# Five upward projections of a two-layer hybrid network as seven quarter products per pair of weight blocks

## What is computed

```python
D_MODEL, SEQ, D_FF = 1024, 512, 4096
def hybrid_layer(x, ...):
    ...
    x = x + merged @ w_o
    h2 = rmsnorm(x, norm_mlp)
    return x + jnp.square(jax.nn.relu(h2 @ w_up)) @ w_down
```

## Time and profile before

| what | value |
|---|---|
| median of 3 runs | 2454.3 us (2454.13 to 2454.35) |
| span of the profiled execution | 2451.9 us |
| PE busy | 2440.2 us, 11368 matmuls |
| DVE / ACT / POOL busy | 1275.7 / 839.2 / 1369.9 us |
| HBM read | 244.17 MB |

### The profile page before, as it was taken

One profiled execution on the slowest core, in us unless ns is written; L12 is line 12 of the kernel. 1 busy time (PEld: TensorE's weight loads), 2 busy tenths in 40 slices (PEclk: granted clock), 3 DMA queues, 4 the chain that ended last, 5 costly groups with the idle time before them and its releaser, 6 DMA issues.

```text
span 2451.9 us, 33111 instructions
## 1 busy us (share of the span) xinstructions
PE 2440.2 (100%) x11368; PEld 1997.5 (81%) x11368; DVE 1275.7 (52%) x1813; ACT 839.2 (34%) x1099; POOL 1369.9 (56%) x1672
## 2 busy tenths in 40 slices
PE   9999999999999999999999999999999999999999
PEld 7888888888888888888888888888777777888887
DVE  7884412355655658844123535437876565733333
ACT  5332232231111223312322312114577775422222
POOL 6556655556766655566555666656432334555554
PEclk9999999999999999999999999999999999999999
DMA  5223332343344332233333433443211212332322
GB/s 192 83 69 98 99 94 94 94 150 127 118 146 146 94 95 86 68 96 94 95 102 95 146 119 125 149 154 95 76 50 42 61 40 70 95 103 87 103 93 93
DMA packets 64887, 247.46 MB, mean 101 GB/s; under 512 B 7200, under 2 KB 9888, under 8 KB 63520
## 3 DMA queue, kind: packets, MB, share of 16 engines
q1 hardware_dynamic: 62496, 218.13, 28.8%
q10 hardware_dynamic: 2304, 28.17, 2.9%
HBM read 244.17 MB, written 2.10 MB: 100 GB/s over the span
## 4 chain that ended last, share of the span: by engine, by line
PE 68%; POOL 16%; issue 12%; DVE 2%; ACT 1%; DVEq 0%; DMA 0%; POOLq 0%; SPq 0%; ACTq 0%
PE ps L586 63%; POOL w_lo L521 16%; PE ps L873 1%; PE ps L886 1%; PE ps L902 1%; PE ps L841 1%; ACT prob L1377 0%; PE ps L906 0%; PE ps L702 0%; DMA w_raw<-weights 0%; DVE sq_q L2036 0%; PE ps L856 0%; DVE A_hi_f L1632 0%; ACT prob L1383 0%; PE ps L778 0%
## 5 line engine op out<-in xcount | busy, mean ns | idle before, releaser
L521 POOL TENSOR_TENSOR w_lo<-w_raw,w_hi 128x256 fp32r<-128x256 f32 x1608 | 1324.4, 855 | 988.4 <-ACT w_hi L1122 855.3
L586 PE MATMUL ps<-H_hi,w_hi 128*128 128x512 f32 x1936 | 767.0, 396 | 0.3 <-DVE H_lo L1987 0.2
L586 PE MATMUL ps<-H_hi,w_lo 128*128 128x512 f32 x1936 | 754.0, 389 | 0.0
L586 PE MATMUL ps<-H_lo,w_hi 128*128 128x512 f32 x1936 | 753.8, 389 | 0.0
L1122 ACT ACTIVATE w_hi<-w_raw 128x1024 fp32r<-128x1024 f32 x399 | 420.3, 1056 | 894.4 <-PE ps L586 864.3
L586 PEld LDWEIGHTS ps<-H_hi,w_hi 128*128 128x128 f32 x1936 | 363.5, 188 | 81.9 <-issue 9.1
L586 PEld LDWEIGHTS ps<-H_lo,w_hi 128*128 128x128 f32 x1936 | 363.6, 188 | 77.2 <-issue 4.5
L586 PEld LDWEIGHTS ps<-H_hi,w_lo 128*128 128x128 f32 x1936 | 363.4, 188 | 76.7
L586 PE MATMUL ps<-A_lo,w_hi 128*128 128x512 f32 x552 | 214.8, 389 | 0.0
L586 PE MATMUL ps<-A_hi,w_hi 128*128 128x512 f32 x496 | 193.0, 389 | 0.0
L586 PE MATMUL ps<-A_hi,w_lo 128*128 128x512 f32 x496 | 193.0, 389 | 0.0
(11 more groups left out here) (291 smaller groups left out, 2929.1 us busy)
## 6 DMA issues: line engine op xcount, KB each, us to landing
w_raw<-weights SPq DMA_DIRECT2D x403, 512.0 KB, 3.6
mod_w<-mod_weights ACTq DMA_DIRECT2D x8, 3072.0 KB, 12.5
toeplitz<-biases SPq DMA_DIRECT2D x14, 128.0 KB, 2.1
out<-X SPq DMA_DIRECT2D x7, 256.0 KB, 2.0
X<-x SPq DMA_DIRECT2D x3, 512.0 KB, 7.8
decay_sb<-decay ACTq DMA_DIRECT2D x1, 1024.0 KB, 7.2
ctx_sb<-context ACTq DMA_DIRECT2D x1, 1024.0 KB, 15.6
X<-x SPq DMA_DIRECT2D x2, 256.0 KB, 4.3
```

The costliest lines, as they stand in the source:

```text
L521: last = nc.gpsimd.tensor_tensor(lo[:, c:c + LOW_COLS], w_raw[:, q, c:c + LOW_COLS], hi[:, c:c + LOW_COLS].bitcast(F32), ALU.subtract)
L586: mm = nc.tensor.matmul(dst, w[l], xs[r], start=start and a == 0, stop=stop and a == 2)
```

## The change

In the five groups (0,1), (0,2), (0,3), (1,1) and (1,2) the eight up jobs become four pairs. The two weight blocks of a pair are a matrix of 2x2 quarters (two output tiles by two halves of the contraction: `A11`, `A12` from the first block, `A21`, `A22` from the second), and `H` is one as well (two halves of the contraction by two halves of the tokens). The pair's product is made from seven quarter products in place of eight (Winograd's form of Strassen's method). A quarter product is 4 tiles times 3 matmuls of 128x256. It needs:

- four sums of weight quarters, `S1` to `S4`, 128x512 each, on DVE (`sum_of`); each of the seven pieces `A11 S3 S2 S4 A12 S1 A22` is rounded by ACT and its low part is made by POOL (five of them, `piece_lows`) or DVE (`S1`, `S3`, `sum_low`);
- four sums of quarters of `H`, `T1` to `T4`, made once for each layer during the up jobs of the group (L,0) (`t_step`): DVE does one 128x1024 difference, twelve 128x256 sums and four 128x1024 low parts, ACT eight 128x256 scalings and four 128x1024 roundings. They lie where `C` was, so that all groups but (1,3) now write to `A`;
- three copies out of PSUM or within it by ACT for each pair (`copy_first`, `keep_second`, `keep_third`, 128x256), and on DVE two 128x256 additions, two instructions that apply relu and `rstd`, and two low parts; the squares move from DVE to ACT (four 128x512 instructions for each pair).

The product of a pair lies in banks n mod 4, the next one, and bank 4 or 7 (`THIRD_BANK`). Since bank 7 is among the banks of the transposes, PE now waits for `mod_reduced` before the first quarter product of such a group. The pieces of the group's first pair are made during the down jobs of the group before (`first_pair`), in the ring slots that those jobs give free. The code and data of the other stages stay.

```diff
+FAST = ((0, 1), (0, 2), (0, 3), (1, 1), (1, 2))
+FAST_JOBS = {L * LAYER_JOBS + JOB_FF + g * FF_GROUP_JOBS + 2 * j: (L, g, j)
+             for L, g in FAST for j in range(DT // 2)}
...
+        def free_of(engine, piece, n):
+            j, i = FAST_JOBS[n][2], PAIR_OF[n]
+            if j == 0:
+                engine.wait_ge(jobs_done, n + place(piece, i) // 2 + 1)
+            elif piece == "S4":
+                engine.wait_ge(jobs_done, n + 2)
+            else:
+                engine.wait_ge(piece_used[piece], i)
...
+            def piece_lows(piece, n):
+                i = PAIR_OF[n]
+                s = place(piece, i)
+                whole = raw_of(piece, n) if piece[0] == "A" else set_lo_f[:, s, :]
+                if piece == "S2":
+                    pool.wait_ge(piece_summed["S4"], i + 1)
+                if piece == "A22":
+                    pool.wait_ge(w_hi_ready, n + 2)
+                else:
+                    pool.wait_ge(piece_high[piece], i + 1)
+                for c in range(0, V_WIDE, LOW_COLS):
+                    last = nc.gpsimd.tensor_tensor(set_lo[:, s, c:c + LOW_COLS], whole[:, c:c + LOW_COLS],
+                                                   set_hi[:, s, c:c + LOW_COLS].bitcast(F32), ALU.subtract)
...
+            def quarter(piece, n, dst, B, start=False):
+                i = PAIR_OF[n]
+                s = place(piece, i)
+                if piece == "A22":
+                    pe.wait_ge(w_lo_ready, n + 2)
+                else:
+                    pe.wait_ge(piece_low[piece], i + 1)
+                for k in range(HALF_K):
+                    cols = slice(k * P, (k + 1) * P)
+                    mm = product(dst, (set_hi[:, s, cols], set_lo[:, s, cols]), B(k), start and k == 0, k == HALF_K - 1, True)
...
+                if part == 1:
+                    pe.wait_ge(bank_free, n + 2)
+                    quarter("A11", n, c11, B11, start=True)
+                elif part == 7:
+                    quarter("S3", n, c21, T(T3), start=True)
+                elif part == 6:
+                    pe.wait_ge(first_copied, i + 1)
+                    quarter("S2", n, c12, T(T2))
+                elif part == 2:
+                    pe.wait_ge(first_copied, i + 1)
+                    quarter("A12", n, c11, B21)
+                elif part == 5:
+                    pe.wait_ge(second_kept, i + 1)
+                    quarter("S1", n, c12, T(T1))
+                elif part == 4:
+                    pe.wait_ge(third_kept, i + 1)
+                    quarter("A22", n, c21, T(T4))
+                else:
+                    pe.wait_ge(c22_added, i + 1)
+                    quarter("S4", n, c12, B22)
...
+                    if (L, g) in FAST:
+                        if g == 1:
+                            pe.wait_ge(t_ready, 4 * (L + 1))
+                        pe.wait_ge(mod_reduced, L * FF_GROUPS + g)
+                        pairs = [ng + 2 * j for j in range(DT // 2)]
+                        for j, m in enumerate(pairs):
+                            fast_pair(m, 1)
+                            fast_pair(m, 7)
+                            if j:
+                                fast_pair(m - 2, 4)
+                            fast_pair(m, 6)
+                            if j:
+                                fast_pair(m - 2, 3)
+                            fast_pair(m, 5 if j == DT // 2 - 1 else 2)
+                            fast_pair(m, 2 if j == DT // 2 - 1 else 5)
+                        fast_pair(pairs[-1], 4)
+                        fast_pair(pairs[-1], 3)
+                        down_part(ng + DT, 0, 6, hi, lo, ready)
+                        down_part(ng + DT + 1, 0, 6, hi, lo, ready)
+                        down_part(ng + DT, 6, DT, hi, lo, ready)
+                        down_part(ng + DT + 1, 6, DT, hi, lo, ready)
...
+                def t_diffs():
+                    V.tensor_tensor(T_lo_f[:, T1, :, :], X[:, 0:HALF_K, HALF_T:S], X[:, 0:HALF_K, 0:HALF_T],
+                                    ALU.subtract).then_inc(diff_ready, 1)
+                def t_sums(t):
+                    dve.wait_ge(diff_scaled, 2 * L + (1 if t == T3 else 2))
+                    fence()
+                    half = slice(0, HALF_T) if t == T4 else slice(HALF_T, S)
+                    for k in range(HALF_K):
+                        last = V.scalar_tensor_tensor(out=T_lo_f[:, t, k, :], in0=X[:, HALF_K + k, half],
+                                                      scalar=column(PAR_NORM2 + HALF_K + k, L),
+                                                      in1=T_lo_f[:, {T3: T3, T2: T1, T4: T2}[t], k, :],
+                                                      op0=ALU.mult, op1=ALU.subtract)
+                    last.then_inc(t_whole, 1)
+                def t_lows(t):
+                    dve.wait_ge(t_high, 4 * L + (2, 3, 1, 4)[t])
+                    V.tensor_tensor(T_lo[:, t, :, :], T_lo_f[:, t, :, :], T_hi[:, t, :, :].bitcast(F32),
+                                    ALU.subtract).then_inc(t_ready, 1)
+                def t_step(s):
+                    if s == 0:
+                        t_diffs()
+                    elif s == 1:
+                        t_sums(T3)
+                    elif s == 2:
+                        t_sums(T2)
+                        t_lows(T3)
+                    elif s == 3:
+                        t_sums(T4)
+                        t_lows(T1)
+                    elif s == 5:
+                        t_lows(T2)
+                    elif s == 6:
+                        t_lows(T4)
...
+                def sum_of(piece, n):
+                    i = PAIR_OF[n]
+                    s = place(piece, i)
+                    a11, a12 = (w_raw[:, n % RING, h * V_WIDE:(h + 1) * V_WIDE] for h in range(2))
+                    a21, a22 = (w_raw[:, (n + 1) % RING, h * V_WIDE:(h + 1) * V_WIDE] for h in range(2))
+                    if piece == "S3":
+                        for b in range(n, n + 2):
+                            dve.wait_ge(w_loaded[b % RING], (b // RING + 1) * 16)
+                    else:
+                        fence()
+                    free_of(dve, piece, n)
+                    a, b, op = {"S3": (a11, a21, ALU.subtract), "S2": (a22, set_lo_f[:, place("S3", i), :], ALU.subtract),
+                                "S4": (a12, set_lo_f[:, place("S2", i), :], ALU.subtract),
+                                "S1": (a21, a22, ALU.add)}[piece]
+                    V.tensor_tensor(set_lo_f[:, s, :], a, b, op).then_inc(piece_summed[piece], 1)
+                def sum_low(piece, n):
+                    i = PAIR_OF[n]
+                    s = place(piece, i)
...
+                def add_c22(n):
+                    i = PAIR_OF[n]
+                    dve.wait_ge(third_kept, i + 1)
+                    dve.wait_ge(piece_used["S1"], i + 1)
+                    V.tensor_tensor(second_out[:, HALF_T:S], ps[:, n % RING + 1, 0:HALF_T], kept[:, 1, :],
+                                    ALU.add).then_inc(c22_added, 1)
...
+                def second_of(n):
+                    i = PAIR_OF[n]
+                    dve.wait_ge(piece_used["A22"], i + 1)
+                    V.tensor_tensor(second_out[:, 0:HALF_T], ps[:, THIRD_BANK[i % 2], 0:HALF_T], kept[:, 0, :],
+                                    ALU.add).then_inc(c21_added, 1)
+                    fence()
+                    V.scalar_tensor_tensor(out=E[:, 1, :], in0=second_out[:, :], scalar=0.0, in1=rstd[:, :],
+                                           op0=ALU.max, op1=ALU.mult).then_inc(bank_free, 1)
...
+                def first_of(n):
+                    q = n % RING
+                    dve.wait_ge(jobs_done, n + 2 + RING)
+                    V.scalar_tensor_tensor(out=halves(E[:, 0, :]), in0=ps[:, q:q + 2, 0:HALF_T],
+                                           scalar=0.0, in1=halves(rstd[:, :]), op0=ALU.max,
+                                           op1=ALU.mult).then_inc(bank_free, 1)
...
+                def fast_low(n, t):
+                    m = 2 * FAST_JOBS[n][2] + t
+                    dve.wait_ge(e_squared, 2 * PAIR_OF[n] + 2 - t)
+                    V.tensor_tensor(A_lo[:, m, :], Alf[:, m, :], A_hi[:, m, :].bitcast(F32),
+                                    ALU.subtract).then_inc(tiles_ready, 1)
...
+                def fast_up(n0):
+                    for j in range(DT // 2):
+                        n = n0 + 2 * j
+                        more = j + 1 < DT // 2
+                        if j:
+                            add_c22(n - 2)
+                            sum_of("S1", n)
+                        if more:
+                            sum_of("S3", n + 2)
+                        if j:
+                            sum_low("S1", n)
+                            second_of(n - 2)
+                        if more:
+                            sum_of("S2", n + 2)
+                            sum_of("S4", n + 2)
+                            sum_low("S3", n + 2)
```

(22 more changed lines are left out.)

258 lines of the change are left out of this document (239 added, 19 removed).

## The result

The changed kernel takes 2495.0 us (median of 4 runs, 2493.8 to 2495.9) against 2454.3 of the kernel before: ratio 1.0167 [1.0152, 1.0181]. The prediction was 2488.0, in 2460 to 2510, slower with 0.86. The span of the profiled execution is 2491.7 us, 39.8 more than before.

What follows compares the result with a forecast made beforehand. The prediction took the kernel to be bound by TensorE's (PE's) stream. On the profiled 2451.9 us, -17.7 + 21.1 + 17.5 + 13 = +33.9 gave a 2485.8 us span, 2488.2 with the runs' extra 2.4; range 2460 to 2510.

Steps and rivals of the forecast that it cites:

- The gain: PE in the 20 pairs: 84 narrow matmuls in place of 48 wide ones save 0.88 us a pair, 17.7 us.
- The rival that ended faster: Quarter products: matmuls under 0.113 us apart would make the kernel faster, 2443.6 us at 0.1067; chance 0.07.
- The wait at the start: Start of the five groups: PE waits for `mod_reduced` behind DVE's added `S1` work, 4.3 or 4.1 us each, 21.1 us.
- DVE inside the up stage: Middle pairs: DVE needs 11.5 us against PE's 10.00 and falls behind; stalls of 3.5 us a group, 17.5 us.
- The prediction's own sign of being wrong: It is wrong if PE does not idle at group starts, or DVE has a free microsecond in the middle pairs.
- The `T` sums: (0,0) and (1,0): DVE's seventeen added instructions make PE stall in its first down job, 6.5 us a layer, 13 us.
- The clock: Rival: granted clock falls to 1.2 GHz for as long as each of five holes lasts, +10.5 us, 2499; chance 0.14.
- DVE keeps pace: Rival: two-input DVE instructions take 0.69 us throughout, only the start waits stay whole, 2464.5 us; chance 0.22.

Runs made afterwards that it cites:

- e11_load_in_gap: Changed kernel with PE's start wait one pair later, `T` low parts and `T4` in down stages, steps reordered, `mod_w` load after the last up block's work: 2443.5 us.
- b2_hole_long: Kernel before, with PE waiting for the reductions at five group starts and DVE's first reduction done three times over: 2485.0 us.
- e4_half_pool: Changed kernel with POOL making only half of the low part of its five pieces, PE using that half twice: 2485.3 us.
- e8_load_last: Changed kernel with PE's start wait one pair later, `T` low parts in down stages, two order swaps, `mod_w` load at the last pair: 2463.7 us.
- b1_hole_short: Kernel before, with PE waiting for DVE's reductions at the start of the same five groups, products as they were: 2466.1 us.
- e1_wait_later: Changed kernel with PE's wait for the reductions moved from ahead of a group's first pair to ahead of its second: 2484.9 us.
- e3_both: Changed kernel with PE's wait for the reductions one pair later and the four `T` low parts moved into the down stages: 2471.4 us.

## Why the prediction was right, and where its steps were not

The account of the changed kernel, with e11_load_in_gap for the gain: -15.3 + 18.5 (holes at the starts) + 10.8 (stalls in up stages, 9.4 of it the two large ones in each) + 8.2 (lower clock there) + 17.6 (down stages of (L,0)) = +39.8. The prediction was -17.7 + 21.1 + 17.5 + 13 = +33.9.

- **The gain**, 17.7: 15.3 by the clean kernel. The spacing was taken from the right row, 0.119 for 0.120 us, which is 1.5 of the missing 2.4; most of the rest is a few single steps of up to 0.22 us in each stage. The rival that ended faster needed 0.113 and falls with it.
- **The wait at the start**, 21.1: right in place, mechanism and order, 3.8 and 3.6 us each for 4.3 and 4.1, 18.5 in all. The five hand-overs came to 0.35 us for the 0.5 set, and the `S1` sum and low part both took the short 0.69. It was called more than the gain alone, and it is: b2_hole_long costs 31 us by holes of that length alone.
- **DVE inside the up stage**, 17.5: the step that failed. The prediction had 11.5 us of DVE work for PE's 10.0 in a middle pair, let DVE fall behind by 1.5 us in each of two, and made 3.5 us of stalls a group out of it. The work was nearly right: 11.05 us in the third pair of e11_load_in_gap. Luck has a part in that. The twelve durations there add up to 11.3 us, where 11.5 less the hand-overs is 10.3; and the hand-overs, set at 1.2, come to -0.2, since eight of the twelve instructions start up to 0.08 us before the end of the one ahead and four some 0.09 behind it. The lag is there too, 3.3 us at the fourth pair. What failed is the step from lag to stall: with the load and the order moved PE does not wait once, so it has that much slack. The stalls that there were, 10.8 us, stand behind the 19th and the 24th product, where PE waits for `first_of` and `keep_second`. Their place in the order is just in time, and contention turns it to late: either less of POOL (e4_half_pool) or another order (e8_load_last behind the 19th product, e11_load_in_gap behind the 24th too) takes them away. The prediction's own sign of being wrong came as well: in (0,1) of the changed kernel DVE was idle for 1.9 us in the second pair and 1.4 in the third.
- **The `T` sums**, 13: waits of PE of 11.4, between the bounds of 5.6 and 24.4 and near the 13, in three waits a layer and not one, and another 6.2 us through the lower clock, 17.6 in all. The seventeen instructions took 14.6 and 15.1 us, inside the 12.7 to 22.1.
- **The clock**, nothing in the sum and 10.5 in its rival: it fell. The rival's condition came true, the prediction put 0.14 on it. It costs some 8.2 us at the starts and 6.2 in (L,0), 14.4 for 34.1 us at the lower level, 0.42 each, and b2_hole_long gives 0.41. That it would cost half the length of a hole was a guess, 10.5 for the 8.2 at the starts; the waits in (L,0) were not counted as a cause at all.
- **DVE keeps pace**, 2464.5, rival: its condition, 0.69 us throughout, did not come true (means of 0.94 and 1.12 in the changed kernel). e11_load_in_gap shows that PE can go on without a stall even so, but not in the order that was written, and the rival left out the clock as well.

So 2488 was near 2495 in part by luck. Its holes and stalls together were 10.9 us too high (2.6 at the starts, 6.7 in the up stages, 1.6 for the `T` sums), the clock's 14.4 were left out, and the gain was put 2.4 too high: +5.9 in sum.

**Still open.** How many of the changed kernel's in-up stalls are order and how many are contention can't be split; each alone is enough to remove most of them. Nor is it known why one hole of 1.9 us in b1_hole_short brought the lower clock and the four others did not. The waits of 2.1 to 3.1 us in e1_wait_later and e3_both are as mixed: four of ten brought it.

## What to carry to other kernels

A saving of PE time pays only when every wait that it uncovers is cleared too: here the same seven-for-eight scheme was 1.7% slower as written, and 0.4% faster with one wait, one load and some steps moved and no arithmetic changed. When a wait goes, look in the trace for what was late under its cover (a load, in e1_wait_later), and look again after each edit, since a reorder on the engine that issues a load moves the load. Count a hole of PE at its length, and look at the granted clock behind it: each microsecond at the lower level costs 0.4 us more.

## What was not expected of the hardware

- A 512 KB load that takes 3 to 5 us took 6 to 13 when a 3 MB load on another engine's queue went out 0.1 us behind it or up to 3 us ahead of it. A shift of 1.2 us between two queues moved a whole kernel by 34 us.
- Holes of 3.3 to 4.0 us brought the granted clock from 2.4 to 1.2 GHz ten times out of ten, in kernels in which PE is otherwise busy for 98 and 99%; waits of 2.1 to 3.1 us four times out of ten, holes of 1.9 us once in three and those of 1.5 never in two.
- Most DVE instructions that wait for nothing start some 0.08 us before the end of the one ahead: twelve in a row took 11.05 us where their durations add up to 11.3.
